# Second halves only: 64 of 128 streamed columns in the doubling levels and pair products of a hybrid decoder layer

## What is computed

```python
# HGRN2: scores of a chunk, decay per channel k
dec = jnp.exp(jnp.where(causal, la[t] - la[s], NEG_BIG))
scores = jnp.einsum('bnthk,bnshk,bntshk->bnhts', q, k, dec)
# gated delta net: unit lower triangular solve, 64 rows a chunk
A = jnp.where(strict, beta[..., :, None] * kk * dec, 0.0)
M = A + jnp.eye(B_CHUNK)
W = lax.linalg.triangular_solve(M, rhs, left_side=True, lower=True, unit_diagonal=True)
```

## Time and profile before

| | us |
|---|---|
| median of 3 runs | 4009.47 |
| lowest, highest | 4003.7, 4012.91 |
| span of the profiled execution | 3988.8 |
| pair stage of the first layer, first L909 to the end of the last feature tile | 159.2 to about 231 |
| levels of the first layer, first L1119 to the end of the last L1132 | 302 to 381.2 |
| the same of the second layer | 2277.6 to about 2353.4 |

### The profile page before, as it was taken

The page is one execution under the profiler, slowest core; times in us unless marked ns, Lnnn a source line. Parts: engine busy times, 40 slices in busy tenths (PEclk is TensorE's granted clock), DMA queues, the critical chain, the costliest instruction groups (busy, mean ns, idle before and its releaser), DMA issues.

```text
span 3988.8 us, 59456 instructions
## 1 busy us (share of the span) xinstructions
PE 3877.4 (97%) x23204; PEld 3461.4 (87%) x23204; DVE 2869.6 (72%) x4841; ACT 1540.6 (39%) x2349; POOL 2259.3 (57%) x1452
## 2 busy tenths in 40 slices
PE   8999999999999999999999999999999999999999
PEld 6778599999999999999477876999999999999994
DVE  5764368955887878888567552799458887798885
ACT  1443145553333334444314432555532333343343
POOL 0032069887777657668101310888877774688861
PEclk9988999999999999999999899999999999999999
DMA  4201146666899999999221021566679899999992
GB/s 122 52 13 48 43 170 215 214 233 218 305 322 320 316 361 388 395 395 343 78 66 39 12 75 43 188 214 210 220 246 312 304 322 333 346 383 380 378 340 71
DMA packets 417975, 900.99 MB, mean 226 GB/s; under 512 B 94496, under 2 KB 242208, under 8 KB 416032
## 3 DMA queue, kind: packets, MB, share of 16 engines
q1 hardware_dynamic: 272288, 552.91, 40.2%
q0 software_dynamic: 90112, 268.76, 18.7%
q10 hardware_dynamic: 55296, 75.52, 5.2%
HBM read 773.87 MB, written 123.15 MB: 225 GB/s over the span
## 4 chain that ended last, share of the span: by engine, by line
PE 52%; POOL 15%; DMA 14%; DVE 11%; issue 5%; ACT 2%; SPq 0%; DVEq 0%; ACTq 0%; POOLq 0%
PE banks L1364 11%; PE banks L826 7%; PE banks L1376 7%; POOL peer_gates L2079 6%; PE banks L1438 5%; DMA u_stage<-peer_ut 5%; POOL u_stage L2095 4%; PE banks L1473 4%; DMA gated<-dense_gelus 3%; PE banks L1275 3%; POOL u_stage L2087 3%; DMA peer_gates<-peer_v,u_stage 3%; PE banks L1293 3%; DVE normed L2729 2%; DMA normed<-peer_ut 1%
## 5 line engine op out<-in xcount | busy, mean ns | idle before, releaser
L2079 POOL DMA_INDIRECT peer_gates<-peer_v,u_stage x512 | 733.8, 1433 | 387.3 <-DVE normed L2729 157.6
L1438 PE MATMUL banks<-gated_parts,v_parts 128*128 128x320 f32 x6144 | 911.1, 310 | 19.9 <-DVE gated_parts L2776 18.2
L1438 PEld LDWEIGHTS banks<-gated_parts,v_parts 128*128 128x128 f32 x6144 | 905.8, 189 | 25.4 <-issue 25.2
L1364 PE MATMUL banks<-peer_x_parts,u_parts 128*128 128x448 f32 x3168 | 664.0, 367 | 3.3 <-DVE u_parts L2715 3.3
L1364 PEld LDWEIGHTS banks<-peer_x_parts,u_parts 128*128 128x128 f32 x3168 | 590.5, 188 | 49.6 <-DVE u_parts L2715 4.1
L2095 POOL DMA_INDIRECT u_stage<-dense_gelus,u_stage x256 | 374.5, 1463 | 106.9 <-issue 77.4
L1364 PE MATMUL banks<-peer_x_parts,low_s 128*128 128x448 f32 x1696 | 398.3, 367 | 0.5 <-DVE low_s L2715 0.5
L2729 DVE SCALAR_TENSOR_TENSOR normed<-peer_gates,u_stage,normed 128x1024 f32<-128x1024 f32 x254 | 327.5, 1289 | 85.3 <-DMA peer_gates<-peer_v,u_stage 71.0
L2745 DVE SCALAR_TENSOR_TENSOR peer_gates<-peer_gates,u_stage 128x1024 f32<-128x1024 f32 x254 | 325.4, 1281 | 81.3 <-DMA peer_gates<-peer_v,u_stage 71.3
L1869 ACT ACTIVATE u_stage<-banks 128x448 f32<-128x448 f32 x256 | 139.2, 544 | 621.8 <-PE banks L1364 616.8
L2087 POOL DMA_INDIRECT u_stage<-gelus,u_stage x256 | 329.0, 1285 | 78.1 <-issue 78.0
(11 more groups left out here) (355 smaller groups left out, 6642.6 us busy)
## 6 DMA issues: line engine op xcount, KB each, us to landing
v_stage<-peer_v SPq DMA_DIRECT2D x256, 512.0 KB, 7.7
u_stage<-peer_ut SPq DMA_DIRECT2D x244, 512.0 KB, 5.2
dense_gelus<-u_stage ACTq DMA_DIRECT2D x256, 224.0 KB, 5.3
gates<-peer_gates SPq DMA_DIRECT2D x16, 2560.0 KB, 20.3
u_stage<-gates SPq DMA_DIRECT2D x64, 640.0 KB, 8.9
gated<-dense_gelus SPq DMA_DIRECT2D x256, 160.0 KB, 7.6
x<-peer_ut SPq DMA_DIRECT2D x64, 512.0 KB, 4.7
u_raw<-peer_ut SPq DMA_DIRECT2D x64, 512.0 KB, 4.9
```

The lines of the kernel that those rows point to most:

```text
L1364: ins = mm(PS[:, d % 2, 0:DW], u_part(n, a, k), XR[:, b, k, DENSE0:TOK], start=(k == 0 and m == 0), stop=(k == KT - 1 and m == 2))
L1438: ins = mm(vc[k][:, 0:PW3], VR[:, s, b, k * 128:(k + 1) * 128], HR[:, s, a, :], start=(j == 0 and m == 0), stop=(j == NKEYS - 1 and m == 2))
L2079: eng.indirect_dma_start(out=GU[:, t % 4, :], out_offset=None, in_=din["peer_v"].rearrange("l i j d -> (l i j) d"), in_offset=bass.Indirec ...
```

## The change

In the pair products of levels 0 to 6 and in both matmuls of doubling levels 1 to 6, only the columns of second halves are streamed: 64 of 128 in a prompt tile, 32 of 64 in the sample tile, read with a stride (runs of 1 << l) and written packed. The stationary operands are as before. ACT's copy of P, DVE's subtraction and DVE's masked copies take the halved width, the DVE ones with strided outputs. A unit's four prompt tiles fill one bank where they filled two, so DVE copies by head instead of by pair of tiles, after all four tiles. The plain units, the transposes, the masking by POOL and all stages between are as before.

```diff
     def unit_banks(u):
         l, c, T = unit_of(u)
-        return 3 if T == TOK else 2
+        return 3 if l is None else 2 if T == TOK else 1
+
+    def second_halves(t, l):
+        w = 1 << l
+        if len(t.shape) == 2:
+            return t.rearrange("p (n g w) -> p n g w", g=2, w=w)[:, :, 1, :]
+        return t.rearrange("p h (n g w) -> p h n g w", g=2, w=w)[:, :, :, 1, :]
+
+    def in_runs(t, l):
+        if len(t.shape) == 2:
+            return t.rearrange("p (n w) -> p n w", w=1 << l)
+        return t.rearrange("p h (n w) -> p h n w", w=1 << l)
...
                     pe.wait_ge(dve_done, at("q_low", L, u))
+                    pe.wait_ge(*bank_free())
+                    b = fill("hsc", L, u, 0).rearrange("p (i h t) -> p i h t", i=4, h=2)
+                    for i in range(SAMPLE):
+                        cols = slice(COL[i], COL[i] + 128)
+                        ins = mm(in_runs(b[:, i], l), left[:, c, cols], second_halves(QP[:, c, :, cols], l), start=True, stop=True)
+                    pe.did(ins.then_inc(pe_done, 1), "filled", "hsc", L, u, 0)
+                    if T == TOK:
+                        pe.wait_ge(*bank_free())
+                        b = fill("hsc", L, u, 1)[0:SAM, 0:SAM].rearrange("p (h t) -> p h t", h=2)
+                        ins = mm(in_runs(b, l), left[:, c, SEQ:TOK], second_halves(QP[:, c, :, SEQ:TOK], l), start=True, stop=True)
+                        pe.did(ins.then_inc(pe_done, 1), "filled", "hsc", L, u, 1)
+                    return
...
                     if l:
-                        ins = mm(b[0:R, h, 0:R], below, XI[0:R, i, h, 0:R], start=True, stop=True)
+                        ins = mm(in_runs(b[0:R, h, 0:R // 2], l), below, second_halves(XI[0:R, i, h, 0:R], l), start=True, stop=True)
...
-                    ins = mm(b[0:R, h, 0:R], TI[0:R, i, h, 0:R], PI[0:R, slot, h, 0:R], start=True, stop=True)
+                    ins = mm(b[0:R, h, 0:R // 2], TI[0:R, i, h, 0:R], PI[0:R, slot, h, 0:R // 2], start=True, stop=True)
...
-                        act.did(A(PI[0:R, n % RING, :, 0:R], b[0:R, :, 0:R], ACT.Copy).then_inc(act_done, 1), "drained", "pi", L, i, l)
+                        act.did(A(PI[0:R, n % RING, :, 0:R // 2], b[0:R, :, 0:R // 2], ACT.Copy).then_inc(act_done, 1), "drained", "pi", L, i, l)
...
                     dve.wait_ge(dve_done, at("drained", "hsc", L, u - 2, unit_banks(u - 2) - 1))
+                    ups = second_halves(const("ups")[:, l * 128:(l + 1) * 128], l).bitcast(U32)
+                    dve.wait_ge(pe_done, at("filled", "hsc", L, u, 0))
+                    b = bank("hsc", L, u, 0).rearrange("p (i h t) -> p i h t", i=4, h=2)
+                    for hh in range(2):
+                        ins = eng.copy_predicated(second_halves(ST[:, :, 2 * c + hh, :], l), bc(ups, 1, 4), in_runs(b[:, :, hh], l))
+                        dve.did(ins.then_inc(dve_done, 1), *(("drained", "hsc", L, u, 0) if hh else ()))
...
-                    dve.did(TT(x_next, x_next, b[0:R, :, 0:R], ALU.subtract).then_inc(dve_done, 1), "drained", "dx", L, i, l)
+                    x_new = second_halves(x_next, l)
+                    dve.did(TT(x_new, x_new, in_runs(b[0:R, :, 0:R // 2], l), ALU.subtract).then_inc(dve_done, 1), "drained", "dx", L, i, l)
```

More of the change, by code:

```diff
@@ L910, in pair_scores @@
                     pe.did(ins.then_inc(pe_done, 1), "filled", "hsc", L, u, two)
[L911 to L915, removed]
+                pe.wait_ge(*bank_free())
+                b = fill("hsc", L, u, 2)[0:SAM, 0:2 * SAM].rearrange("p (h t) -> p h t", h=2)
+                ins = mm(b, left[:, c, SEQ:TOK], QP[:, c, :, SEQ:TOK], start=True, stop=True)
+                pe.did(ins.then_inc(pe_done, 1), "filled", "hsc", L, u, 2)
             def decayed_turned(i):
@@ L2022, in _ @@
             pool.wait_ge(act_done, at("vt", L))
-            pool.wait_ge(pe_done, at("filled", "hsc", L, HUNITS - 1, 1))
+            pool.wait_ge(pe_done, at("filled", "hsc", L, HUNITS - 1, 0))
             for h in range(4):
@@ L2358, in chosen @@
                     dve.wait_ge(dve_done, at("drained", "hsc", L, u - 2, unit_banks(u - 2) - 1))
+                    ups = second_halves(const("ups")[:, l * 128:(l + 1) * 128], l).bitcast(U32)
[4 more added lines that the diff above has]
+                        dve.did(ins.then_inc(dve_done, 1), *(("drained", "hsc", L, u, 0) if hh else ()))
+                    if T == TOK:
+                        ups = second_halves(const("ups")[0:SAM, l * 128:l * 128 + SAM], l).bitcast(U32)
+                        dve.wait_ge(pe_done, at("filled", "hsc", L, u, 1))
+                        b = bank("hsc", L, u, 1)[0:SAM, 0:SAM].rearrange("p (h t) -> p h t", h=2)
+                        ins = eng.copy_predicated(second_halves(SST[0:SAM, 2 * c:2 * c + 2, :], l), bc(ups, 1, 2), in_runs(b, l))
+                        dve.did(ins.then_inc(dve_done, 1), "drained", "hsc", L, u, 1)
+                    return
                 for two in range(unit_banks(u)):
@@ L2369, in chosen @@
                         over = lambda m: bc(m[0:SAM, 0:SAM], 1, 2)
[L2370 to L2374, removed]
+                    dve.did(TT(out, b, over(ident), ALU.mult).then_inc(dve_done, 1), "drained", "hsc", L, u, two)
             def conv(c):
@@ L2416, in _ @@
             counts.same(("conv", L), ("qr_ready", L, 5))
-            counts.same(("hst", L), ("drained", "hsc", L, HUNITS - 1, 1))
+            counts.same(("hst", L), ("drained", "hsc", L, HUNITS - 1, 0))
             step_state(0)
```

## The result

The changed kernel takes 4077.24 us in the median of four runs (4068.84 to 4093.67) against 4009.12 (four runs): 1.0178 of before, 95% interval 1.0138 to 1.0218. Slower, by 68 us; forecast were 4097, 4030 to 4114.

What follows compares the result with a forecast made beforehand. TensorE was taken to bound the pair stage and the levels. From the profiled 3988.8 us, less 19 for the pair stage, plus 107 for levels at half clock, plus 20.7 put back, came 4097; range 4030 to 4114.

Steps and rivals of the forecast that it cites:

- Pair stage: Pair products: 128 columns instead of 256 save 0.107 us each, 8.6 + 0.3 + 0.6 = 9.5 us a layer, 19 for both.
- The chain on ACT: Pair stage's end: ACT's last exponential, 0.62 us late behind DVE, starts sooner as DVE's copies shorten; 0.6 us a layer.
- DVE's copies: Pair stage's masked copies: 256 elements instead of 512 take 429 ns each, and DVE does not become the bound.
- rival D: Pair stage: strided columns stream slowly, so it gives 2 us instead of 19; 4114 with half-clock levels; chance 0.04.
- Levels at full clock: Doubling levels at clock 1.00: the 128-wide weight load sets the pace, 0.111 us, so 64 columns gain nothing.
- Levels and the clock: Doubling levels: short streams keep the 0.50 clock at which they are entered, 0.214 us a load; costs 52 and 55 us.
- the factor 0.93: Levels: 0.214 / 0.111 - 1, the extra share of busy time at half clock; 54.3 and 57.7 us before idle is subtracted.
- Putting back the 20.7 us: Whole program: the profiled 3988.8 us lies 20.7 under the median of 4009.5, added at the end to reach 4097.5.
- A: The forecast itself: half clock through the levels of both layers, 4097 us; chance 0.50.
- B: Levels: clock returns part-way, behind a head norm next to transposes; 23 us a layer, 4036 or 4066; chance 0.22.
- C: Levels: clock rises as before, 1.00 by about 310, so they cost nothing; 3990 us; chance 0.18.
- E: Levels: weight loads do not slow at half clock, so 64 columns pace near 0.111; 3980 us; chance 0.03.

Runs made afterwards that it cites:

- level 1 whole: Changed kernel with level 1's products, copy and subtraction put back to 128 columns, levels 2 to 6 still halved; ratio 1.0036 to the kernel before.
- the right product halved: Changed kernel with each level tile's first product and ACT's copy back at 128 columns, only the second product halved; ratio 0.9993 to the kernel before.
- levels only: Kernel before with only the doubling levels halved, pair products as before; ratio 1.0152, and 1.0110 when run again.
- pairs only: Changed kernel with the doubling levels put back to 128 columns, only the pair products halved; ratio 0.9977, and 0.9943 when run again.
- the second set: The changed kernel run again without any edit; ratio 1.0194 to the kernel before.
- the 32 transposes: Changed kernel, all levels halved, with 32 transposes of 128 columns that compute nothing added ahead of level 1's first product; ratio 1.0049 to the kernel before.
- levels 1 and 5 whole: Changed kernel with levels 1 and 5 put back to 128 columns, levels 2, 3, 4 and 6 still halved; ratio 0.9986 to the kernel before.

## Why the prediction was right, point by point

**Pair stage.** L921 takes 0.12 each, forecast 0.111: the 80 on the path save 80 x (3.49 - 1.92) / 16 = 7.9 us, not 8.6, and the sample matmuls and the tail must have given the rest, which no run shows apart. The last feature tile came 9.0 us earlier, the sums of squares L1011 9.7 (242.9 to 233.2), and two profiles against two give 9.5 a layer: the term held. The chain on ACT ran as told. The first exponential of the last unit waits no more, and the drain comes 9.8 us earlier than in the earlier trace rows:

```profile
223.93 0.42 ACT L1665 ACTIVATE mixers<-mixers 128x256 f32<-128x256 f32 x1
...
232.20 0.64 ACT L1675 ACTIVATE mixers<-banks 128x256 f32<-128x256 f32 x2
```

**DVE's copies** were mis-sized at the low levels. I took 429 ns for all of them:

```profile
172.33 1.36 DVE L2387 COPY_PREDICATED mixers<-kept,banks 128x256 f32<-128x256 uint32 x2 [0.50 <-PE banks L921]
...
223.10 0.82 DVE L2387 COPY_PREDICATED mixers<-kept,banks 128x256 f32<-128x256 uint32 x2 [0.98 <-PE banks L921]
```

At level 0 a copy of 256 takes 0.68 us, hardly less than one of 512 (0.74 in the mean), and as much at level 1; at level 3 it is 0.51, at level 5 0.41. It costs nothing in the time, since DVE still waits for L921, 6.0 us in all. For TensorE, rival D, there is no such price: at level 0 eight loads of L921 take 1.15 and 1.01 us, at level 5 sixteen take 2.00.

**Levels at full clock: nothing to gain.** Held: 0.111 for 64 columns in the levels themselves (level 1 whole), and the right product halved left the mixers as they were.

**Levels and the clock.** The mechanism held: never released, 0.214 a load. But the reading "entered at half clock" began a microsecond late. The first loads of level 1 in the kernel before:

```profile
301.98 0.97 PEld L1119 LDWEIGHTS banks<-mixers 128*128 128x128 f32 x8 [1.53 <-POOL mixers L2066]
303.77 1.78 PEld L1119 LDWEIGHTS banks<-mixers 128*128 128x128 f32 x8 [0.82 <-POOL mixers L2066]
```

The clock was 1.00 from 299.5 to 302.9, right behind level 0's sixteen transposes, and fell after these waits. The changed kernel's first profile had no such stretch, its second had one ahead of either layer's levels; it made no difference in level 1. The size was off. Forecast were 52 and 55 us, measured 49 (levels only, 430.1 against 381.1; changed kernel against pairs only, 420.7 against 371.6). The failed term is the factor 0.93. It takes every load at 0.214, and a tile for 20 x 0.2135 = 4.27 us; measured are 4.16, because a product that stands ahead of the transposes takes 1.60 for its eight instead of 1.71 (339.40 to 341.00 above). Against the 20 x 0.111 = 2.22 of a tile at full clock that is 0.87 more, and the forecast's two sums become 58.4 x 0.87 - 2.6 = 48 and 62.0 x 0.87 - 2.7 = 51, on either side of the 49.

**What was not in it.** The clock is down earlier, too, for 3.4 us at 227.1, in the tail of the pair stage, where short streams now stand between waits. The pairs alone have that dip in one profile, in the other 0.50 on end from 228.8 to 256.1, and still gain their 9.5.

**The sum.** 4097 against 4077 and, in the second set, 1.0194 or 78 us over before, which on 4009 is 4087. Putting back the 20.7 us was sound: the profiled execution of before was a short one, and 4009.5 - 19 + 107 = 4097 adds the change to the median. With the measured 98 in place of 107 it is 4088, which is 1.0197 and inside the first set's interval too. What is left between 4088 and 4077 no run explains; the four executions spread over 25 us.

**The rivals.** A held, and B was no mere rival but what some executions do: in one layer of one of the changed kernel's two profiles, and in one layer of one of the two with only the levels changed. Its price was 23 us a layer; measured are 392.1 - 371.6 = 20.5 and 402.5 - 381.1 = 21.4. The two do not exclude each other, which the chances treated them as doing. C failed at its own test: no 1.00 by 310. It was right in one half, that 64-column streams hold a clock that is there (40.7 us behind the 32 transposes). They do not always: entered at 1.00 in the changed kernel's second profile, with waits of 1.39 and 0.82 us, they lost it and did not bring it back. E failed: 0.214 a load at half clock.

## What to carry to other kernels

Before halving what a matmul streams, read in the timeline of weight loads whether the stream or the load sets the pace, and read the granted clock of the stretch. Behind a 128-wide load, 128 columns cost no more than 64, so a cut from 256 to 128 paid (9.5 us a layer) and one from 128 to 64 could only lose (49 us a layer, mostly). If a dense stage is entered at half clock, or loses the clock in its first gaps, its first long streams are what bring it back: keep them there, even ones that compute nothing, and look at both ends of the stage and behind every short-column step in it.

## What the runs showed of the hardware

- TensorE can be busy 126.15 of 126.30 us and keep 0.50 throughout. Gapless halved levels mostly leave the clock where it is: at 0.50 for 126 us in the profile after, at 1.00 for 40.7 us behind the 32 transposes. With one of the two products whole it rose, 8.0 to 9.1 us after the first product's start.
- Transposes bring the clock. It was 1.00 at 299.5 in the kernel before, right behind sixteen of them from 296.36 on, and 1.00 at 299.9 near the end of the 32 from 293.87 on. Two waits of 1.5 and 0.8 us with eight instructions between them stood ahead of its fall at 302.9.
- The same program can behave in two ways: a layer's levels wholly at 0.50 (mixer 420), or with a return of 34 us (392). It shows as a mean clock of 0.950 to 0.961 over executions of the changed kernel, and 0.953 to 0.972 of the levels alone; a median over few runs mixes them.
- A masked copy on DVE of 256 elements a partition takes 0.68 us when its runs are one or two elements long, 0.51 with eight, and 0.40 with 64 (L2387 at 172.33, 183.09, 204.00 and 227.51 in the profile after).
- In level 6 the clock fell behind a 2.8 us wait of TensorE where the products around it were halved (360.2, in the kernel with levels 1 and 5 whole), and not where they were whole.
